# The last down GEMM of a fused two-block kernel by three fp32r passes, with its remainders subtracted on GpSimd

## What is computed

```python
def conv_ffn(h, w_up, conv_w, conv_b, w_down, rows):
    u = h @ w_up                                   # 256 x 1024 @ 1024 x 5632
    u = dwconv2d_grid(u, conv_w, conv_b, rows)     # 3x3, on a 4 x 64 grid
    a, g = jnp.split(u, 2, axis=-1)
    return (jax.nn.silu(g) * a) @ w_down           # 256 x 2816 @ 2816 x 1024
...
        xl = xl + g2l * conv_ffn(hl, ffn_w_up[layer], ffn_conv_w[layer], ffn_conv_b[layer], ffn_w_down[layer], rows)
...
    return rmsnorm(xl, final_norm_g)
```

## Time and profile before

| | us |
|---|---|
| median of 3 runs | 3139.31 (3137.63 to 3141.06) |
| the profiled execution | 3133.52, its span 3131.7 |
| PE busy | 2798.1 (89%) |
| DVE busy | 1850.6 (59%) |
| ACT busy | 1034.2 (33%) |
| POOL busy | 192.2 (6%), 89 instructions |

### The profile page before, as it was taken

How to read it: one execution, slowest core, us unless ns; L and a number is a source line. 1 busy time by engine, 2 the same in 40 slices (tenths; PEclk the granted TensorE clock), 3 DMA queues, 4 the chain that set the end, 5 groups by cost and what they waited for, 6 DMA issues and landing times.

```text
span 3131.7 us, 47736 instructions
## 1 busy us (share of the span) xinstructions
PE 2798.1 (89%) x18018; PEld 2351.4 (75%) x18018; DVE 1850.6 (59%) x3211; ACT 1034.2 (33%) x1334; POOL 192.2 (6%) x89
## 2 busy tenths in 40 slices
PE   2999989999999998988899557999999799869998
PEld 2998877899999877888778444587744577648887
DVE  5785254676786744588612476477732666661871
ACT  1432132443533123333343552333300544441211
POOL 0000000000000000000034000144300000000000
PEclk9999999999999999999999678999999999969999
DMA  7786632576675832466321101222243211103441
GB/s 254 276 316 253 231 108 103 201 262 267 217 268 205 306 121 95 163 240 234 129 81 68 63 1 43 72 95 94 96 186 141 81 68 56 62 18 120 149 172 70
DMA packets 112961, 468.54 MB, mean 150 GB/s; under 512 B 6984, under 2 KB 64912, under 8 KB 65936
## 3 DMA queue, kind: packets, MB, share of 16 engines
q1 hardware_dynamic: 112784, 466.14, 41.2%
HBM read 465.05 MB, written 1.06 MB: 149 GB/s over the span
## 4 chain that ended last, share of the span: by engine, by line
issue 52%; PE 34%; DVE 6%; DVEq 4%; ACT 3%; ACTq 1%; POOLq 0%; PEldq 0%; PEld 0%
PE accs L765 9%; PE accs L666 3%; PE accs L667 3%; PE accs L668 3%; PE accs L653 2%; DVEq L2542 2%; PE accs L1113 2%; PE accs L1114 2%; PE accs L1115 2%; DVE normed L86 1%; PE mix L1161 1%; ACT arena L76 1%; PE mix L812 1%; PE mix L1152 1%; DVE arena L2519 1%
## 5 line engine op out<-in xcount | busy, mean ns | idle before, releaser
L666 PE MATMUL accs<-normed_r,arena_r 128*128 128x256 f32 (+2 forms) x1864 | 587.4, 315 | 39.0 <-DVEq L1974 24.4
L667 PE MATMUL accs<-arena_r 128*128 128x256 f32 (+1 forms) x2090 | 594.5, 284 | 0.0
L668 PE MATMUL accs<-normed_r,panel_r 128*128 128x256 f32 (+2 forms) x1872 | 585.6, 313 | 0.0
L653 PE MATMUL accs<-normed,panel 128*128 128x256 f32 x2176 | 482.5, 383 | 6.2 <-ACTq L461 3.0
L653 PEld LDWEIGHTS accs<-normed,panel 128*128 128x128 f32 x2176 | 413.3, 191 | 70.1 <-ACTq L461 4.3
L666 PEld LDWEIGHTS accs<-normed_r,arena_r 128*128 128x128 f32 (+1 forms) x1864 | 351.8, 189 | 77.1 <-DVEq L1974 23.9
L667 PEld LDWEIGHTS accs<-arena_r 128*128 128x128 f32 x2090 | 395.2, 189 | 2.2 <-issue 0.2
L1358 ACT ACTIVATE arena_r<-panel 128x1024 fp32r<-128x1024 f32 (+1 forms) x240 | 275.3, 1147 | 326.3 <-DMA panel<-w 114.2
L86 DVE TENSOR_TENSOR panel_r<-panel,arena_r 128x1024 fp32r<-128x1024 f32 (+1 forms) x240 | 319.7, 1332 | 96.2 <-ACTq L1359 54.3
L668 PEld LDWEIGHTS accs<-normed_r,panel_r 128*128 128x128 f32 (+1 forms) x1872 | 351.5, 188 | 24.0
L2519 DVE SCALAR_TENSOR_TENSOR arena<-accs,vectors,arena 128x189 f32<-128x189 f32 (+2 forms) x704 | 279.2, 428 | 95.5 <-issue 65.7
(11 more groups left out here) (371 smaller groups left out, 4140.0 us busy)
## 6 DMA issues: line engine op xcount, KB each, us to landing
panel<-w SPq DMA_DIRECT2D x250, 1024.0 KB, 4.9
panel<-w SPq DMA_DIRECT2D x48, 1408.0 KB, 8.4
cond_panel<-wc SPq DMA_DIRECT2D x60, 1024.0 KB, 6.9
normed<-wc SPq DMA_DIRECT2D x52, 1024.0 KB, 7.3
arena<-wc SPq DMA_DIRECT2D x8, 1024.0 KB, 6.7
residual<-xs SPq DMA_DIRECT2D x2, 1024.0 KB, 6.9
residual<-crows SPq DMA_DIRECT2D x2, 512.0 KB, 8.8
constants<-cond_row_kept SPq DMA_DIRECT2D x2, 512.0 KB, 4.4
```

Source lines behind the costliest of these rows:

```text
L653: mm = pe.matmul(acc[b][:, o:o + ntok], w[:, k * PANEL + j * P:k * PANEL + j * P + P], rhs(k), start=(k == 0), stop=(k == KD - 1))
L666: pe.matmul(out, hi[:, k, 0:m], src_hi(k), start=clear and k == 0, stop=False, skip_group_check=True)
L667: pe.matmul(out, hi[:, k, 0:m], src_lo(k), start=False, stop=False, skip_group_check=True)
L668: mm = pe.matmul(out, lo[:, k, 0:m], src_hi(k), start=False, stop=last and k == n - 1, skip_group_check=True)
```

## The change

`down1` becomes a split GEMM. PE runs 33 matmuls for a half panel in place of 11 fp32 products, each behind a `low_made` of that half. ACT makes the high part of each of the 16 half panels (`down_high`, 128x1408) into a ring of four tiles, POOL the remainders (`low`). `hid` is split too: ACT copies each pair of feature tiles to fp32r (`hid_high`, 128x512) ahead of the middle taps of a later panel, POOL subtracts in place (`hid_low`). Half panels of panels 0 and 1 are made at panels 20 and 21 of `up1`; those of panels 2 to 7 behind the last `gated` and `hid_low` on POOL, and behind the last `silu` and `hid_high` on ACT, and so ahead of `rms_norm` on ACT. DVE and SP have the same instructions as before.

```diff
@@ plan
-        order += [Gemm(f"up{l}", 22, both, split=(l == 0), kept=(l == 0)), Gemm(f"down{l}", 8, both, wide=True, panels_per_acc=2, ahead=BANKS // both)]
+        order += [Gemm(f"up{l}", 22, both, split=(l == 0), kept=(l == 0)),
+                  Gemm(f"down{l}", 8, both, wide=True, panels_per_acc=2, ahead=BANKS // both, split=(l == 1), kept=(l == 1))]
...
+        down1_hi = [region(off, KSPLIT, P, of=arena_r) for off in (UC + 4096, UC + 4096 + KSPLIT * P, UC + 4096 + 2 * KSPLIT * P, 11264)]
+        hid1 = region(0, KF, 2 * T, of=arena_r)
+        hid1_hi, hid1_lo = hid1[:, :, T:2 * T], hid1[:, :, 0:T]
...
@@ PE
+            def last_down(norm):
+
+                g = G["down1"]
+                for i, (n, part) in enumerate(g.parts):
+                    a = g.a0 + n
+                    b = a % BANKS
+                    if i % BANKS == 0:
+                        pe.wait_ge(S("hid_ready"), 44 + (KF // 2 if part else (KSPLIT + 1) // 2))
+                    if part == 0:
+                        pe.wait_ge(free[b], a // BANKS)
+                    for j in range(2):
+                        split_half(g, 0, i, j, acc[b][:, j * T:j * T + T],
+                                   lambda k: hid1_hi[:, part * KSPLIT + k, :], lambda k: hid1_lo[:, part * KSPLIT + k, :],
+                                   part == 0 and j == 0, part == 1, (first_used, ready[b] if part else half_read)[j])
+                    if part == 1 and n >= 1:
+                        rms_sums(norm, range(2 * n - 2, 2 * n), T)
...
@@ POOL
-            def gated(it, u):
-
-                if u % 2 == 1:
+            def gated(par, k, count):
+
+                pool.wait_ge(S("up_silu"), count)
+                pool.tensor_tensor(hid[:, k, 0:T], uconv[:, par, 0:2, 0:T], uconv[:, par, 2:4, 0:T], ALU.mult)
+                pool.drain().then_inc(S("up_used"), 1)
+
+            def hid_low(k, count):
+
+                pool.wait_ge(S("h_parts"), count)
+                pool.tensor_tensor(hid1_lo[:, k, :], hid[:, k, 0:T], hid1_hi[:, k, :], ALU.subtract)
+                pool.drain().then_inc(S("hid_ready"), 1)
+
+            def last_up(it, u):
+
+                static = isinstance(it, int)
+                if u % 2 == 1 and not (static and it == 0 and u == 1):
                     par = u // 2
...
+                    gated(1 - par, slice(2 * par - 2, 2 * par) if static and it == 0 else bass.ds(it * 4 + (2 * par - 2), 2), it * 2 + (11 + par))
+                    if not (static and it == 0):
+                        hid_low(bass.ds(it * 4 + (2 * par - 4), 2), it * 2 + (24 + par - 1))
+                if static and it == 5:
+                    low(G["down1"], 0, u)
+
+            groups(pool, G["up1"], last_up, peel=True)
+            gated(0, slice(20, 22), 22)
+            for pair in (9, 10):
+                hid_low(slice(2 * pair, 2 * pair + 2), 24 + pair + 1)
+            for i in range(2, 8):
+                low(G["down1"], 0, i)
...
@@ ACT
+                def hid_high(k):
+
+                    act.eng.activation(hid1_hi[:, k, :], hid[:, k, 0:T], ACT.Copy)
+                    act.drain().then_inc(S("h_parts"), 1)
+
+                def down_high(i):
+
+                    d = G["down1"]
+                    s = (d.p0 + i) % SLOTS
+                    act.wait_ge(landed[s], 16 * ((d.p0 + i) // SLOTS + 1))
+                    for j in range(2):
+                        if i >= 2 and j == 0:
+                            act.wait_ge(first_used, G["evengate"].s0 + 12 + i - 1)
+                        elif 2 <= i < 6:
+                            act.wait_ge(half_read, d.h0 + i - 1)
+                        elif i >= 6:
+                            wait_ready(act, d, 0, i - 6)
+                        elif (i, j) == (1, 1):
+                            wait_ready(act, G["up1"], 5, 1)
+                        act.eng.activation(split_parts(d, i, j)[0], half_panel(d, i, j), ACT.Copy)
+                        act.drain().then_inc(S("high_made"), 1)
...
                         if u % 2 == 0 and j == 0 and not (isinstance(it, int) and it == 0):
                             act.wait_ge(S("up_used"), it * 2 + (11 * l + par - 1))
+                            if l == 1:
+                                hid_high(bass.ds(it * 4 + (2 * par - 4), 2))
...
+                    if l == 1 and isinstance(it, int) and it == 5:
+                        down_high(u)
...
                 silu(0, 11 * l + 11)
+                if l == 1:
+                    for pair in (9, 10):
+                        act.wait_ge(S("up_used"), 11 + pair + 1)
+                        hid_high(slice(2 * pair, 2 * pair + 2))
+                    for i in range(2, 8):
+                        down_high(i)
```

More of the change, by code:

```diff
@@ L485, in split_parts @@
                 hi = kept_hi[g.name][:, :, j * P:j * P + P]
+            elif g.name == "down1":
+                hi = down1_hi[(2 * u + j) % 4]
             else:
@@ L1307, in _ @@
                 rms += 1
-                down(G[f"down{l}"], rms, lambda k: hid[:, k, 0:ntok], ntok, pairs=11 * l)
+                if l == 0:
+                    down(G["down0"], rms, lambda k: hid[:, k, 0:ntok], ntok, pairs=0)
+                else:
+                    last_down(rms)
             rms_norm(rms, lat)
@@ L1324, in _ @@
                 groups(pool, G[name], lambda it, u, g=G[name]: low(g, it, u))
-            g = G["up1"]
-            def gated(it, u):
-                if u % 2 == 1:
-                    par = u // 2
-                    pool.wait_ge(S("up_silu"), it * 2 + (11 + par + 1))
-                    pool.tensor_tensor(hid[:, bass.ds(it * 4 + u - 1, 2), 0:T], uconv[:, par, 0:2, 0:T], uconv[:, par, 2:4, 0:T], ALU.mult)
-                    pool.drain().then_inc(S("up_used"), 1)
-            groups(pool, g, gated)
+            def gated(par, k, count):
[9 more added lines that the diff above has]
+                if u % 2 == 1 and not (static and it == 0 and u == 1):
+                    par = u // 2
+                    gated(1 - par, slice(2 * par - 2, 2 * par) if static and it == 0 else bass.ds(it * 4 + (2 * par - 2), 2), it * 2 + (11 + par))
[9 more added lines that the diff above has]
+                low(G["down1"], 0, i)
         @block.scalar
```

## The result

| | before | after |
|---|---|---|
| median | 3135.54 us, 9 runs (3132.68 to 3141.06) | 3143.88 us, 9 runs (3141.61 to 3150.18) |
| ratio | | 1.0029, 95% interval 1.0019 to 1.0040 |
| the profiled execution | 3133.52, span 3131.7 | 3143.88, span 3142.1 |
| busy: PE, ACT, POOL | 2798.1, 1034.2, 192.2 us | 2791.6, 1063.5, 257.7 us |

The changed kernel is 0.3% slower: 8.3 us between the medians, 9.1 us by the ratio, 10.4 us between the two spans. The kernel before measured 3135.54 us here and 3139.31 us in the three runs that the prediction started from; the ratio carried over to those is 3148.4 us (3145.3 to 3151.9), beside the forecast of 3149.5. The bare median of after, 3143.88, lies 0.6 us under the forecast's lower end.

A forecast was written before the change was run, and what follows sets the result against it. TensorE in down1 was taken as the bound; its saving of 13.4 us against 23.6 us of waits and slow clock costs 10.2 us, added to the median 3139.31: 3149.5 us, range 3144.5 to 3154.

The forecast's parts named there:

- TensorE's new pace: In down1, 33 matmuls a half panel take 3.93 us, 16 halves 62.9 us instead of 76.3, saving 13.4 us.
- VectorE's late start: At the entry of up1's loop, hid_high ahead of the middle taps delays VectorE by 0.85 us, to its end.
- The remainders of panel 2: Behind the last gated and two hid_low on GpSimd; TensorE starts panel 2 at 3070.17 after some 6 us idle.
- The clock: TensorE restarts at 1.2 GHz behind the waits for panel 2 and the sums, losing 1.94 us each time.
- The squares: Queued on ScalarE behind panel 7's copy and the table load, they keep TensorE waiting about 3.7 us after panel 5.
- rival (1): Behind panel 5, squares are not late and no clock is lost there: +4.3 us, 3143.6; chance 0.07.
- The sum: At the kernel's end, last down1 matmul at 3126.86, 10.2 us later; span 3141.9, median 3149.5; chance 0.70.
- (2): TensorE's clock stays at 2.4 GHz through both waits in down1: +6.3 us, 3145.6; chance 0.13.
- (4): In down1 the waits are hidden after all and the 13.4 us arrive: 3125.9; chance 0.02.
- (3): GpSimd's subtractions of panel 1 stop VectorE's taps, panel 2 starts 6.6 us later: +16.8, 3156.1; chance 0.05.

The follow-up runs named there:

- e4_behind: Changed kernel, but in up1's loop ScalarE copies the pair of hid behind the two middle taps, not ahead of them; 3145.05 us, ratio 1.0030.
- e5_fill: Changed kernel with 18 unused small matmuls in TensorE's wait before panel 2 and 12 in the one before the first sums; 3141.51 us, ratio 1.0018.
- e8_dve2: Changed kernel, but VectorE, not GpSimd, subtracts the remainders of panels 2 to 7; 3143.98 us, ratio 1.0030.
- e1_squares: Changed kernel, but ScalarE loads the Sqrt table and squares output tiles 0 and 1 ahead of panel 7's copies; 3139.96 us, ratio 1.0014.
- e3_both: e1_squares plus panels 2 and 3 made ahead of the last silu and gated, panel 1's remainders ahead of pair 9's gated; 3129.51 us, ratio 0.9983.
- e10_turn: e9_best, but VectorE begins panel 4's subtractions only when GpSimd has done the last hid_low; 3121.29 us, ratio 0.9962.
- e9_best: e7_dve4 plus e4_behind's order, panel 0's copies ahead of panel 20's middle taps, panel 4's ahead of the last hid_high; 3127.38 us, ratio 0.9974.
- e11_pool: e9p_pool, but hid_high stands behind the two middle taps of its panel, as in e4_behind; 3125.41 us, ratio 0.9977.
- e9p_pool: e3_both with panel 0's and panel 4's copies moved ahead as in e9_best, all remainders on GpSimd; 3124.49 us, ratio 0.9964.
- e7_dve4: e3_both, but VectorE subtracts the remainders of panels 4 to 7; 3126.41 us, ratio 0.9971.

## Why the prediction was right

**TensorE's new pace** was right. Two panels in a row end 7.87 us apart (ScalarE's L1800 rows, released by TensorE, start at 3095.68 and 3103.55): 3.93 us a half panel, as read from `out11` in the earlier trace rows.

**VectorE's late start** was 1.12 us and not 0.85. ScalarE and VectorE at the entry of the loop, as in the earlier trace rows:

```profile
2920.91 0.63 ACT L1783 ACTIVATE arena_r<-arena  x1 [3.94 <-PE accs L660]
2921.77 0.56 ACT L1816 ACTIVATE arena<-accs,vectors 128x256 f32<-128x256 f32 x1 [0.23 <-issue]
2922.84 0.56 ACT L1816 ACTIVATE arena<-accs,vectors 128x256 f32<-128x256 f32 x1 [0.51 <-issue]
```

```profile
2923.60 0.87 DVE L2596 SCALAR_TENSOR_TENSOR arena<-accs,vectors,arena 128x252 f32<-128x252 f32 x2 [1.90 <-ACTq L1818]
...
3054.16 7.55 DVE L2596 SCALAR_TENSOR_TENSOR arena<-accs,vectors,arena 128x189 f32<-128x189 f32 x18 [0.45 <-issue]
```

The 0.27 us more are 0.28 of issue ahead of the second middle tap (0.51, before 0.23). The shift is carried to the end as forecast: against `up1`'s start the last tap ends at 177.70 in place of 176.59. e4_behind took it away again.

**The remainders of panel 2.** The steps were right, and two errors cancelled: 3.16 us for 1408 columns where 3.31 was taken, by proportion (the slope had given 3.26), and 0.18 between two instructions where 0.25 was read in the earlier trace rows, against the later start. TensorE started at 3070.31, the forecast was 3070.17. The wait was 5.19 us ("some 6"), that of panel 1 5.12 ("5"): TensorE was through with panel 1 at 3065.12 and not "near 3064", because the clock behind panel 1's wait stayed low for 5.5 us (3054.59 and two halves of 3.93 would be 3062.45).

**The clock** fell behind the waits for panel 2 and for the sums, as forecast, but for some 3.4 us and not 4.4. Panels 2 to 5 took 33.20 us (3070.31 to 3103.51) against 31.44 without it: 1.8 where 1.94 was taken. Behind the sums, from 3108.50 (3107.05 plus 1.45) to 3126.40, it is 17.90 against 16.58: 1.3. e5_fill shows that it is the clock: with the engine kept at work both stretches shrink by 1.5 us. With the 13.4 us that TensorE's passes save, 22.9 us were lost: some 3 by the clock, the rest by the waits themselves. The Trainium skill's rule that bursts with idle stretches between them begin at the lower clock ("TensorE: Matmul & The Clock Gate", section "HAM oscillation — how this bites in real kernels") agrees with these traces at the waits of 3.54 us and more, but not at the one of 3.39 us in e8_dve2.

**The squares** were late by the steps named. From TensorE's end to the first sum it took 3.54 us (some 3.7), copy, table load, small activation, square one behind the other. e1_squares removed exactly this, and rival (1) is what it measured: 1.0014, +4.2 us by the stretch (237.01 less 232.86), where +4.3 had been reckoned.

**The sum.** The last residual was forecast for 3126.86 and came at 3126.40. The span came at 3142.1, where 3141.9 was forecast, and that closeness is in part luck: the stretch grew by 9.5 us and not by 10.2, and the tail, taken as unchanged, was 0.7 us longer. The median came 5.6 us under the forecast. Of these, 3.8 are the level of the kernel before (3135.54 over nine runs, 3139.31 over the first three); the other 1.9, between 10.2 forecast and 8.3 between the medians, is within the interval of the ratio, 6.0 to 12.5 us. The chances of the three outcomes were not quite the sum of their parts: by these (0.70, half of 0.13, 0.05, 0.03) slower is 0.845 and not 0.82.

**Rivals.** (2), a clock that stays, and (4), hidden waits, are refuted by the trace. (3), VectorE held up by GpSimd's subtractions of panel 1, is refuted for the taps: GpSimd subtracts from 3051.24 to 3054.40 and again from 3054.57, over taps whose last group takes 7.55 us, before 7.54. In e3_both GpSimd subtracts and multiplies with no pause over 0.18 us from 3039.36 until VectorE's taps have ended, and they end at 177.77 from the start of `up1`, in the changed kernel at 177.70. The mechanism of (3) does exist, though, and showed as soon as the VectorE instruction had two SBUF inputs. What I gave 0.05 as a property of the pair of engines is one of the instruction's operands: PSUM, one SBUF tensor and a column of factors do not collide.

**What I had not seen** is how little stood between this change and a gain. The forecast took the order on GpSimd as given ("the order of both engines forbids it"); e3_both moves six remainders, four copies and the squares ahead, and the same three passes come out 0.17% faster than the kernel before; e10_turn, where VectorE takes the last eight remainders, 0.38%.

## What to carry to other kernels

When cheaper passes take the place of dear ones, the operands they need become the path: follow the first product that reads each new operand back through the queue of the engine that makes it, and put ahead of it in that queue only what this product needs. Look at the first instruction of the next stage on every engine too (here a table load and two squares behind a copy that waits for TensorE). And when a second engine is to help, look at both instructions' operands before at their durations: started earlier, it can make both finish later.

## What the runs showed of the hardware

- GpSimd's subtraction of two SBUF tensors takes 1.26 to 1.30 us for 128x512, 2.41 for 128x1024 and 3.15 to 3.26 for 128x1408.
- VectorE's subtraction of 128x1408 (1.63 us alone) and GpSimd's 128x512 (1.28) do not run at once: in e9_best the one ends 1.48 us behind the other's end, and the other 1.12 to 1.15 us behind that. e10_turn, where one line keeps them apart, has 1.62 and 1.28 to 1.30. VectorE's taps with an input from PSUM run beside GpSimd's subtractions at their old length.
- Of TensorE's waits, those of 3.54 to 6.22 us (ahead of panels 1 and 2 and of the sums, in after, e1_squares, e4_behind and e8_dve2, and ahead of panel 1 in e5_fill) are each followed by a phase at 1.2 GHz, 3.1 to 5.5 us long (behind panel 2's wait 3.4 in after and 4.5 in e4_behind, behind panel 1's 5.5 in after). Below that it goes both ways: behind 2.02 (e3_both), 2.03 (e11_pool) and 2.29 us (e9_best), all ahead of panel 4, the clock fell; behind 2.06 us at the same place (e9p_pool), 3.39 us ahead of panel 2 (e8_dve2) and behind 1.96 to 1.99 us at the start of `down1` (after, e1_squares, e4_behind, e5_fill, e3_both, e7_dve4, e8_dve2) it did not. What decides between them stays open. From the start of panel 4 to the last residual it is 33.45 us in e9p_pool and 34.96 in e11_pool: the price of the fall is 1.5 us here too.
- Small matmuls without use, put into a wait, kept the clock up behind it (e5_fill), for 1.5 us each time. Taking the waits away shortened the stretch by 15.5 (e3_both) to 21.5 us (e10_turn).
